# Segment sums of a bidirectional scan: one fp32 product replaced by two fp32r products, both operands built on GpSimd

## The reference, cut to what matters

```
a_cum = cumsum(dt * a) within the chunk                      # per head
seg   = a_cum[:, :, :, None] - a_cum[:, :, None, :]           # (l, s)
decay = exp(where(l >= s, seg, -1e30))
cb    = einsum("bclgn,bcsgn->bclsg", cc, bc)
y_diag = einsum("bclsgr,bcsgrp->bclgrp", cb[..., None] * decay, xdt)
```

## Time and profile before

| | |
|---|---|
| median of 3 runs | 1497.83 us |
| the profiled execution | 1495.38 us |
| its span | 1493.4 us |
| busy: PE / DVE / ACT / POOL | 1351.5 / 826.1 / 480.9 / 153.3 us |
| seg products on PE (L1610) | 50.2 us in 128 records |
| building `rr` on POOL (L818) | 50.9 us in 32 instructions |
| scan of the four groups | about 184 to 560 us |

### The profile page before, as it was taken

One profiled execution on the slowest core, in us unless ns is written; L12 is line 12 of the kernel. 1 busy time (PEld: TensorE's weight loads), 2 busy tenths in 40 slices (PEclk: granted clock), 3 DMA queues, 4 the chain that ended last, 5 costly groups with the idle time before them and its releaser, 6 DMA issues.

```text
span 1493.4 us, 18425 instructions
## 1 busy us (share of the span) xinstructions
PE 1351.5 (90%) x7015; PEld 1039.3 (70%) x7015; DVE 826.1 (55%) x1246; ACT 480.9 (32%) x723; POOL 153.3 (10%) x117
## 2 busy tenths in 40 slices
PE   4599989798997998989999999997889999899998
PEld 1256767476674776657777777775767556799998
DVE  1654487596786655364343353434694333667765
ACT  0532022232222313152122221212632676444442
POOL 2200031210312100400000000023020000300000
PEclk8699999999999999989999999999799899899999
DMA  8275101011110111424444444433432000355554
GB/s 340 111 282 206 43 29 57 15 57 43 43 43 29 57 57 62 158 88 145 162 147 147 147 149 147 171 134 100 114 106 71 15 1 1 113 172 190 187 184 139
DMA packets 47909, 166.60 MB, mean 112 GB/s; under 512 B 12889, under 2 KB 13293, under 8 KB 44653
## 3 DMA queue, kind: packets, MB, share of 16 engines
q1 hardware_dynamic: 47852, 165.84, 32.1%
HBM read 164.77 MB, written 1.05 MB: 111 GB/s over the span
## 4 chain that ended last, share of the span: by engine, by line
PE 69%; issue 14%; DVE 8%; ACT 4%; POOL 2%; DMA 2%; SPq 0%; POOLq 0%; DVEq 0%; ACTq 0%
PE ps L1446 53%; PE ps L1452 3%; PE ps L1610 2%; PE ps L1756 2%; PE ps L1730 2%; ACT u L860 2%; PE ps L1629 2%; DMA mring<-in_w_mod 1%; PE ps L1744 1%; DVE cacc L1202 1%; DVE sq L1130 1%; DVE hent L1256 1%; DVE w_lo L1052 1%; DVE nt L1310 1%; POOL rr L818 1%
## 5 line engine op out<-in xcount | busy, mean ns | idle before, releaser
L1446 PE MATMUL ps<-a_hi,w_hi 128*128 128x512 f32 (+1 forms) x1072 | 407.9, 381 | 46.9 <-DVE a_lo L1142 39.2
L1446 PE MATMUL ps<-a_hi,w_lo 128*128 128x512 f32 (+1 forms) x1072 | 384.3, 359 | 0.0
L1446 PE MATMUL ps<-a_lo,w_hi 128*128 128x512 f32 (+1 forms) x1072 | 384.3, 359 | 0.0
L1052 DVE TENSOR_TENSOR w_lo<-raw,w_hi 128x1024 fp32r<-128x1024 f32 x206 | 260.0, 1263 | 80.1 <-ACT w_hi L830 79.7
L830 ACT ACTIVATE w_hi<-raw 128x1024 fp32r<-128x1024 f32 x206 | 217.2, 1056 | 246.2 <-DMA raw<-in_w_ff 195.6
L1446 PEld LDWEIGHTS ps<-a_hi,w_hi 128*128 128x128 f32 x1072 | 209.2, 195 | 107.4 <-issue 50.0
L1446 PEld LDWEIGHTS ps<-a_lo,w_hi 128*128 128x128 f32 x1072 | 210.2, 196 | 31.0 <-issue 2.4
L1446 PEld LDWEIGHTS ps<-a_hi,w_lo 128*128 128x128 f32 x1072 | 209.2, 195 | 29.3
L1446 PE MATMUL ps<-b_hi,w_hi 128*128 128x512 f32 (+1 forms) x576 | 200.5, 348 | 3.8 <-DVE b_lo L1327 3.8
L1446 PE MATMUL ps<-b_lo,w_hi 128*128 128x512 f32 (+1 forms) x576 | 198.2, 344 | 0.0
L1446 PE MATMUL ps<-b_hi,w_lo 128*128 128x512 f32 (+1 forms) x576 | 198.1, 344 | 0.0
(11 more groups left out here) (196 smaller groups left out, 1399.8 us busy)
## 6 DMA issues: line engine op xcount, KB each, us to landing
raw<-in_w_ff SPq DMA_DIRECT2D x128, 512.0 KB, 3.3
mring<-in_w_mod SPq DMA_DIRECT2D x24, 1024.0 KB, 7.5
mring<-in_w_mod SPq DMA_DIRECT2D x32, 768.0 KB, 5.0
raw<-in_w_in_even SPq DMA_DIRECT2D x36, 512.0 KB, 3.3
raw<-in_w_in_odd SPq DMA_DIRECT2D x18, 512.0 KB, 3.4
raw<-in_w_out_even SPq DMA_DIRECT2D x16, 512.0 KB, 3.3
raw<-in_w_out_odd SPq DMA_DIRECT2D x8, 512.0 KB, 3.2
bias<-in_rpb_na SPq DMA_DIRECT2D x16, 128.0 KB, 3.9
```

What stands on the lines that cost most here:

```text
L1052: v.tensor_tensor(w_lo[:, u % RING, :, :], raw[:, u % RING, :, :], w_hi[:, u % RING, :, :].bitcast(F32), ALU.subtract).then_inc(lo_done, 1)
L1446: ins = mm(out_ap, w_[:, n % RING, k, :], x_[:, k, 0:ntok], start=(k == 0 and j == 0), stop=(k == KT - 1 and j == 2))
```

## The change

The two masks `tgt` and `tlt` are copied once into an fp32r tile `after`. The step logarithms `dta` are split once, on DVE, into a rounded part `dta_hi` and the remainder `dta_lo`. POOL then builds two operands of 128x768 per seg step, `rr_hi` and `rr_lo`, both fp32r, and PE adds four fp32r matmuls of 384 columns where two fp32 matmuls stood. `rr_lo` and the split lie over the Fourier constants, which are dead by then. PE waits for both operands, POOL for the previous seg product.

```diff
+        after = place("after", [P, 2 * P], F32R, offset=c0_at + 4 * 3 * P)
+        rr_lo = place("rr_lo", [P, R, P], F32R, offset=o)
+        dta_hi = place("dta_hi", [P, NCH, 2 * NH], F32R, offset=o + 4 * R * P)
+        dta_lo = place("dta_lo", [P, NCH, 2 * NH], F32R, offset=o + 4 * R * P + 4 * NCH * 2 * NH)
...
                     if n == 0:
-                        pool.wait_ge(dt_done, 1)
+                        pool.wait_ge(dta_split, 1)
                         pool.wait_ge(c0_in, 16)
+                        pool.wait_ge(*filled(("dfts", FN_T - 1)))
                     else:
                         pool.wait_ge(*filled(seg_l[n - 1]))
-                    pool.tensor_tensor(rr[:, :, :],
-                                       dts["dta"][:, ch, NH * di + R * g:NH * di + R * g + R].unsqueeze(2).broadcast_to([P, R, P]),
-                                       (tle, tge)[di][:, None, :].broadcast_to([P, R, P]), ALU.mult).then_inc(rr_done, 1)
+                    for rr, part in ((rr_hi, dta_hi), (rr_lo, dta_lo)):
+                        pool.tensor_tensor(rr[:, :, :],
+                                           part[:, ch, NH * di + R * g:NH * di + R * g + R].bitcast(F32).unsqueeze(2).broadcast_to([P, R, P]),
+                                           (tle, tge)[di][:, None, :].broadcast_to([P, R, P]), ALU.mult).then_inc(rr_done, 1)
...
                             dve.wait_ge(*filled(("dfts", FN_T - 1)))
+                            dve.wait_ge(dtx_done, 3)
+                            v.tensor_copy(after[:, :], c0[:, 3 * P:5 * P]).then_inc(signal(dve_seq), 1)
+                            v.tensor_copy(dta_hi[:, :, :], dts["dta"][:, :, :]).then_inc(signal(dve_seq), 1)
+                            dve.wait_ge(*latest())
+                            v.tensor_tensor(dta_lo[:, :, :], dts["dta"][:, :, :], dta_hi[:, :, :].bitcast(F32), ALU.subtract).then_inc(signal(dta_split), 1)
...
-                    pe.wait_ge(rr_done, seg_n[st] + 1)
+                    pe.wait_ge(rr_done, 2 * seg_n[st] + 2)
...
                     for i in range(2):
-                        ins = mm(ps[:, b + i, 0:GX], (tgt, tlt)[dirs[st[2]]], rr[:, 3 * i:3 * i + 3, :].rearrange("p h l -> p (h l)"),
-                                 start=True, stop=True)
+                        for j, rr in enumerate((rr_hi, rr_lo)):
+                            ins = mm(ps[:, b + i, 0:GX], after[:, P * dirs[st[2]]:P * dirs[st[2]] + P], rr[:, 3 * i:3 * i + 3, :].rearrange("p h l -> p (h l)"),
+                                     start=(j == 0), stop=(j == 1))
```

More of the change, by code:

```diff
@@ L445, in trunk @@
         w_lo = place("w_lo", [P, RING, KT, P], F32R, offset=raw_at)
+        c0_at = at[0]
         c0 = place("c0", [P, C0_W])
@@ L486, in trunk @@
         ey = place("ey", [P, 2, R, P])
-        rr = place("rr", [P, R, P])
+        rr_hi = place("rr_hi", [P, R, P], F32R)
         cbm = place("cbm", [P, 2, P])
@@ L507, in trunk @@
         vf = place("vf", [P, NCH, 2 * P], offset=o + 4096)
+        o = c0_at + 4 * (6 * P)
+        after = place("after", [P, 2 * P], F32R, offset=c0_at + 4 * 3 * P)
+        rr_lo = place("rr_lo", [P, R, P], F32R, offset=o)
+        dta_hi = place("dta_hi", [P, NCH, 2 * NH], F32R, offset=o + 4 * R * P)
+        dta_lo = place("dta_lo", [P, NCH, 2 * NH], F32R, offset=o + 4 * R * P + 4 * NCH * 2 * NH)
         at[0] = out_at
@@ L555, in trunk @@
                  "silc_done th0_done h_done sq_done var_done rstd_done nt_done u_done split_done coef_done "
-                 "wdthi_done wdtlo_done dtv_done dte_done dtln_done dt_done dtx_done uf_done vf_done pad_done acc_done "
+                 "wdthi_done wdtlo_done dtv_done dte_done dtln_done dt_done dta_split dtx_done uf_done vf_done pad_done acc_done "
                  "th_done xbc_done xdt_done xw_done ent_done rr_done seg_done g_done y_done zt_done gate_done gated "
@@ L563, in trunk @@
          consts_set, vt_done, silc_done, th0_done, h_done, sq_done, var_done, rstd_done, nt_done,
-         u_done, split_done, coef_done, wdthi_done, wdtlo_done, dtv_done, dte_done, dtln_done, dt_done, dtx_done,
+         u_done, split_done, coef_done, wdthi_done, wdtlo_done, dtv_done, dte_done, dtln_done, dt_done, dta_split, dtx_done,
          uf_done, vf_done, pad_done, acc_done, th_done, xbc_done, xdt_done, xw_done, ent_done, rr_done, seg_done,
```

## The result

The changed kernel takes **1512.25 us** in the median (1507.94 to 1516.73, 5 runs) against 1497.83 before (1497.32 to 1499.75, 5 runs): 1.0087 times as long, interval 1.0069 to 1.0105. It is slower by 14 us. The forecast was 1511, and slower at 0.79. The profiled execution took 1508.9 us, its span is 1507.1 (before 1495.38 and 1493.4). The trace of the kernel before, at 0.954, is of a quick one.

The account below looks back on a forecast made before the run. PE looked the bound, but DVE, held up by POOL's builds, had no room in groups 1 and 2 and little in group 0. Terms 0.85 + 6.0 + 5.1 + 4.1 - 2.9 = +13.2 gave 1511 us, range 1498 to 1521.

Parts of the forecast that it names:

- the hidden parts: Groups 1 and 2: build time not stopping DVE, 0.9 under exp, 2.2 under the reciprocal, 1.5 under ycomb and cbm.
- The seg product: PE, each scan step: four records 0.17 apart, 0.70 instead of 1.29, gain 0.59 per step, 18.9 us over 32.
- DVE and POOL in turn: Scan: SBUF instructions of both exclude each other whole, L1202 and L1215 included; maxima near 2.2, DVE busy about 30 more.
- Rival 2: Scan: only forms seen held up count, L1202 and L1215 run beside a build; about -6, 1492; chance 0.08.
- The price of a hold: Convolution part: each unhidden build stops DVE for its whole 1.47; group 0 ey 7.4 later, PE +4.4.
- The end of group 0: Last seg step, no tile ahead: release to y product a chain of 6.4 instead of 5.03, +1.36.
- The clock: Behind PE's added waits matmuls run at 1.2 GHz: +2.0 in group 0, +1.0 in group 1; group 2 includes such a term.
- By groups: Scan: group 0 +6.0, group 1 +5.1, group 2 +4.1, group 3 -2.9, with 0.85 for the split ahead.
- The split: Ahead of toks: three small DVE instructions splitting dta, hidden by nothing, +0.85 (0.6 to 1.1).
- The first step of a group: First seg step of each group: second build ends about 0.4 after PE is ready, +0.4 four times.
- The split of the mixed output: Group 3: rr_lo goes in turn between DVE's ey and first a_lo, which PE waits for, +1.47.
- Rivals 1, 3, 4: PE decides everywhere, 1484, chance 0.04; fp32r slow to write on POOL, 1526, 0.06; losses and gains cancel, 1498, 0.10.

Follow-up runs that it names:

- experiments 1, 2 and 6: Changed kernel without the rr_lo build, 1482.96 us; kernel before with its build done twice, 1527.92; changed kernel with each build in six pieces, 1525.46.
- experiments 10 and 11: Changed kernel with both operands built by ScalarE, behind the tanh and next w_hi, 1491.92 us; kernel before with its one build there, 1490.25.
- b1: Kernel before, fp32 product kept, with POOL building a second tile that nobody reads and PE waiting for both: 1527.92 us, ratio 1.020.
- a1: Changed kernel without the build of rr_lo, PE multiplying the rounded tile twice: 1482.96 us, ratio 0.990.

## Why the prediction was right, step by step

The sign, the place and the mechanism were right, and the sum +13.2 met +13.7 in the profile. Two of its terms were off in opposite directions, so the closeness of the sum is partly luck. A slip is in it too: in groups 1 and 2 the hidden parts, 0.9, 2.2 and 1.5, leave 10.1 of 14.7 and not 9.8, which would have made the sum 13.8.

**The seg product.** In 24 of the 32 steps its records are 0.17 to 0.18 apart, as forecast. In the other 8 they are 0.32 apart, at the lower clock.

**DVE and POOL in turn.** Right, L1202 and L1215 with them: maxima of 1.84 and 1.77, DVE busy +26.5 (forecast 2.2 and +30). Here the trace agrees with the rule of the Trainium skill (SBUF — State Buffer, Who interferes with whom). The first tap, a form with one tensor, is held too (1.84 at most before). Rival 2 falls with these maxima, and experiments 1, 2 and 6 show that the turns are what costs.

**The price of a hold.** This was the first mis-sized term. I charged DVE with the whole build, 1.47. A held tap or gate is up to 1.09 or 1.07 longer. The tap issued at 208.57 shows why: the build takes the turn at 208.54 and ends at 209.87, 1.33 later, and the tap is done 0.55 behind it, though it takes 0.75 alone. So 0.14 of the build's time and 0.20 of the tap's pass while they wait. The longest hold of the scan is 1.28 (`hent` L1270, 1.84 instead of 0.56). In group 0 `ey` for the second y product is done at 233.74, 5.55 later than before, of which 1.1 are the split; the forecast was 7.4 and, ahead of it, 0.85 for the split. PE's wait there is 2.98, not 4.4. In groups 1 and 2 the cover by PSUM-fed instructions was judged about right: 3.92 at the third y product (forecast 4 to 5), 2.63 and 2.84 at the last chunk (about 3).

**The end of group 0.** The chain of seven links was right, its length not: from the release to the y product's weights 7.3 us instead of the forecast's 6.4, and 5.03 before. From the start of the seg product to that of the exponential behind it went 1.75 (259.87 to 261.62) instead of 1.05 (255.18 to 256.23, one step earlier): the lower clock.

```profile
256.21 1.47 POOL L827 TENSOR_TENSOR rr_hi<-dta_hi,c 128x768 fp32r<-128x768 f32 x1 [6.74 <-PE ps L1625]
256.23 0.81 ACT L950 ACTIVATE ey<-ps 128x768 f32<-128x768 f32 x1 [4.36 <-PE ps L1625]
257.64 2.18 POOL L827 TENSOR_TENSOR rr_lo<-dta_lo,c 128x768 fp32r<-128x768 f32 x1
...
261.62 0.81 ACT L950 ACTIVATE ey<-ps 128x768 f32<-128x768 f32 x1 [4.58 <-PE ps L1625]
...
263.48 2.75 PEld L1644 LDWEIGHTS ps<-xdt,ey 128*128 128x128 f32 x24 [0.54 <-DVE ey L1284]
```

**The clock.** This was the second: 2 + 1 + 1 = 4 us forecast, 16 by the account of the two traces, and some 3 less for typical executions, since the medians over all of them lie 44 apart where the two traced ones lie 50. I had looked for it only behind the waits that I added, on the y product. The stretches from one group to the next, which I took as unchanged, show it too, the first and the third (all three had a clock of 0.91 before; after):

```profile
268.57:291.41 22.84, 15.21 (x32) 6.75 (x32) 12.77 (x22) 3.46 (x3) 8.65 (x8) 0.68 0.00 0
372.91:392.81 19.90, 11.49 (x32) 5.12 (x32) 12.63 (x22) 3.45 (x3) 8.62 (x8) 0.91 0.00 0
477.24:497.88 20.64, 12.22 (x32) 5.30 (x33) 12.63 (x22) 3.45 (x3) 8.61 (x8) 0.83 0.00 0
```

Before they were 19.44, 19.71 and 19.73. The change touches nothing in them but the first builds of the next group, and they cost 4.5 us. PE waits 0.25 for `rr_lo` in two of them, and 0.75 longer for `hent` in the first; the rest is the clock.

**By groups.** Up to the end of group 0 +4.95 (forecast 6.85, split included), group 1 +5.9 (5.1), group 2 +5.8 (4.1), group 3 -2.8 (-2.9); behind it nothing. Too much for the holds, too little for the clock.

**The split.** `xw` starts 1.1 us later (forecast 0.85, bounds 0.6 to 1.1). **The first step of a group** waits 0.25, three times (forecast 0.4, four times). **The split of the mixed output** makes PE wait 4.39 for `a_lo`, 1.08 more (forecast 1.47): again the price of a hold.

**Rivals 1, 3, 4.** PE doesn't decide everywhere; a build is not slower for its fp32r output (1.47); gains and losses didn't cancel in the changed kernel, though between experiments 10 and 11 they do.

## What to carry to other kernels

Before work goes to an engine with idle time, ask which instructions of its neighbour it shuts out, and count each as a hold of up to one build (1.1 to 1.3 us here for a build of 1.47), not as free. Where PE is the bound, write three columns, its waits, half the time at the lower clock outside of them, and the rest: a product made cheaper shows up in the third and can be lost in the other two. A gap in PE ahead of a wait that can't go may be worth filling with products that nobody reads. Before two clocks are compared, look at what executions of one kernel differ by.

## What the runs showed that I had not expected

- 128 products without any use, 32 at each group, put into two gaps, made the kernel 4 us faster than the version without them (1483.53 against 1487.62, each about 1499.5 for the kernel before), and cut a group of six products from 5.12 to 2.84 us. In the kernel before the same six take 4.25; whether filling its gaps pays too was not tried.
- GpSimd writing 128x768 with zeros takes 0.74 us and takes no turn with DVE's forms of two tensors, but does with its TENSOR_SCALAR (2.15 instead of 0.55, build and fill in a row); reading and writing the same size takes 1.47 and takes turns with both.
- Small pieces are dear: 128x128 takes 0.39 us on GpSimd (a sixth of a build would be 0.25) and 0.39 on ScalarE with a scale of its own for each partition, where 128x256 took 0.38 without one. In a row they come every 0.36 and 0.30 us.
- At two builds a step, both products had 75 us at 1.2 GHz in the scan (after, b1). At one build two traces had 32 and 58 (before, a1), but over all executions the medians of the whole program lie only 9 apart: one trace of each doesn't settle such a difference.
